# Differential attention: the tail's norm in two groups of heads, the projection begun with six heads, and items two rounds behind the units

## What is computed

```python
qkv = jnp.einsum('bld,de->ble', x, w_in)
q, k, v = jnp.split(qkv, 3, axis=-1)        # 8 heads; q and k in two halves of 64, v of 128
...
s = jnp.einsum('bqhcd,bkhcd->bhcqk', qblk, k) * scale
s = s - slopes[None, :, None, None, None] * dist
p = jax.nn.softmax(s, axis=-1)
a = p[:, :, 0] - lam * p[:, :, 1]
o = jnp.einsum('bhqk,bkhe->bqhe', a, vf)
...
o = o * lax.rsqrt(jnp.mean(o * o, -1, keepdims=True) + SUBLN_EPS) * subln_g * (1.0 - lam_init)
return jnp.einsum('ble,ed->bld', o, w_o)
```

## Time and profile before

| | |
|---|---|
| time, median of 3 runs | 2782.74 us (2771.02 to 2784.29) |
| time of the profiled execution | 2781.65 us |
| its span in the trace | 2779.6 us |
| TensorE / VectorE / ScalarE busy | 94% / 73% / 55% |
| start of the scores of item 21, the first behind the last unit | 120.34 us |
| start of the projection | 150.87 us |
| end of the projection, start of the norm's sums | 177.04 us |

### The profile page before, as it was taken

How to read it: one execution, slowest core, us unless ns; L and a number is a source line. 1 busy time by engine, 2 the same in 40 slices (tenths; PEclk the granted TensorE clock), 3 DMA queues, 4 the chain that set the end, 5 groups by cost and what they waited for, 6 DMA issues and landing times. The chain is left out here.

```text
span 2779.6 us, 48273 instructions
## 1 busy us (share of the span) xinstructions
PE 2601.0 (94%) x20505; PEld 2138.3 (77%) x20505; DVE 2017.6 (73%) x2876; ACT 1534.7 (55%) x2217; POOL 128.9 (5%) x176
## 2 busy tenths in 40 slices
PE   8899999998997999999999999998999889999888
PEld 7689987787965666666666666666969779979778
DVE  7755558654356989889898989896757865757864
ACT  5544425221124877777777778775446444546443
POOL 0000000010004000000000000000200101100101
PEclk9999999999997999999999999999999999999999
DMA  6325433100033989899999989893625534625532
GB/s 193 97 73 185 162 117 116 61 4 3 4 135 118 367 331 365 332 347 349 345 351 347 350 330 365 332 365 105 197 74 167 175 104 145 196 76 167 166 105 101
DMA packets 250985, 550.43 MB, mean 198 GB/s; under 512 B 25549, under 2 KB 193157, under 8 KB 207629
## 3 DMA queue, kind: packets, MB, share of 16 engines
q1 hardware_dynamic: 246796, 541.52, 56.1%
q0 software_dynamic: 3968, 5.78, 0.7%
HBM read 540.43 MB, written 1.05 MB: 195 GB/s over the span
## 5 line engine op out<-in xcount | busy, mean ns | idle before, releaser
L316 DVE TENSOR_TENSOR wl<-raw,wh 128x1024 fp32r<-128x1024 f32 (+1 forms) x610 | 742.6, 1221 | 341.8 <-ACT wh L307 324.1
L307 ACT ACTIVATE wh<-raw 128x1024 fp32r<-128x1024 f32 (+1 forms) x610 | 640.5, 1053 | 485.0 <-PE PS L163 434.0
L316 DVE TENSOR_TENSOR wl<-early,wh 128x1024 fp32r<-128x1024 f32 x384 | 466.8, 1225 | 55.6 <-ACT wh L307 35.3
L307 ACT ACTIVATE wh<-early 128x1024 fp32r<-128x1024 f32 x384 | 407.0, 1061 | 128.0 <-PE PS L163 118.7
L161 PE MATMUL PS<-wh,xe_h 128*96 128x512 f32 x896 | 357.2, 399 | 1.2 <-DVE xe_l L2018 1.2
L161 PE MATMUL PS<-b_hn_h,wh 128*128 128x256 f32 (+1 forms) x1152 | 336.9, 292 | 22.1 <-DVE wl L316 15.9
L163 PE MATMUL PS<-wh,xe_l 128*96 128x512 f32 x896 | 353.6, 395 | 0.0
L162 PE MATMUL PS<-wl,xe_h 128*96 128x512 f32 x896 | 353.6, 395 | 0.0
L162 PE MATMUL PS<-b_hn_l,wh 128*128 128x256 f32 (+1 forms) x1152 | 329.6, 286 | 0.0
L163 PE MATMUL PS<-b_hn_h,wl 128*128 128x256 f32 (+1 forms) x1152 | 329.4, 286 | 0.0
L161 PEld LDWEIGHTS PS<-b_hn_h,wh 128*128 128x128 f32 (+1 forms) x1152 | 223.0, 194 | 28.4 <-DVE wl L316 18.3
(11 more groups left out here) (473 smaller groups left out, 5046.8 us busy)
## 6 DMA issues: line engine op xcount, KB each, us to landing
early<-in_moe_in SPq DMA_DIRECT2D x128, 1024.0 KB, 5.0
raw<-in_moe_in SPq DMA_DIRECT2D x96, 1024.0 KB, 4.9
raw<-in_w_in SPq DMA_DIRECT2D x76, 1024.0 KB, 5.4
early<-in_moe_out SPq DMA_DIRECT2D x64, 1024.0 KB, 4.9
raw<-in_moe_out SPq DMA_DIRECT2D x48, 1024.0 KB, 5.0
raw<-in_attn_w_in SPq DMA_DIRECT2D x24, 512.0 KB, 5.8
raw<-in_rw_w_rkv SPq DMA_DIRECT2D x12, 1024.0 KB, 5.0
raw<-in_ffn_w_gate SPq DMA_DIRECT2D x11, 1024.0 KB, 5.5
```

The source lines that it names most:

```text
L307: act.e.activation(st.two(n)[0], st.raw(n), ACT.Copy).then_inc(*act.sig("hi", st.name, n, sem=f"hi_{st.name}"))
L316: dve.e.tensor_tensor(lo, st.raw(n), hi.bitcast(F32), SUB).then_inc(*dve.sig("lo", st.name, n, sem=f"lo_{st.name}"))
```

## The change

It has three parts. First, items run two rounds behind the units, not three: n = i - 2, with `unit(i)` written ahead of `scores(n)`, and the loop is three rounds shorter in its count. Second, the norm over heads is done in two groups: heads 0 to 5 (bank 6, `n_0`, `r_0`), whose root is taken while items 22 and 23 are still at work, and heads 6 and 7 (bank 7, `n_1`, `r_1`), whose root is taken during the projection. Third, the projection starts when the first rows of group 0 are there; the sum of squares of head 7 stands behind its first row of the contraction, the spreads of heads 6 and 7 behind its fifth. The four unused matmuls go, and PSUM banks are named by hand.

```diff
--- before.py
+++ after.py
@@ -528,7 +528,7 @@
     at_t = [tile3(f"at_t{n}", 3, T) for n in range(2)]
     at_x = [tile(f"at_x{n}", 8) for n in range(NP_)]
     lam_m, lam = tile("lam_m", 64), tile("lam", 4)
-    at_sq, n8, r8 = tile3("at_sq", KC, T), tile("n8", T)[0:8], tile("r8", T)[0:8]
+    at_sq, n8, r8 = tile3("at_sq", KC, T), *([tile(f"{x}8_{g}", T)[0:8] for g in (0, 1)] for x in "nr")
     at_xs = two("at_x", KC, T)
     at_u = [tile(f"at_u{n}", T) for n in range(2)]
     ITEMS = [(h, i) for h in range(8) for i in range(3)]
@@ -536,19 +536,19 @@
     def attention_order(unit, v_turned, scores, turned, values, sums):
 
 
-        for i in range(len(UNITS) + 8):
-            n = i - 3
+        for i in range(len(UNITS) + 5):
+            n = i - 2
+            if i < len(UNITS):
+                unit(i)
             if 0 <= n < len(ITEMS):
                 scores(n)
-            if i < len(UNITS):
-                unit(i)
             if i >= 3 and i % 3 == 0 and i <= len(UNITS):
                 v_turned(i // 3 - 1)
             if n >= 5 and n % 3 == 2 and n // 3 <= 8:
                 values(n // 3 - 1)
             if 2 <= n < len(ITEMS) + 2:
                 turned(n - 2)
-            if n >= 7 and n % 3 == 1 and n // 3 <= 9:
+            if n >= 7 and n % 3 == 1:
                 sums(n // 3 - 2)
 
     def attention_pe(pe):
@@ -609,25 +609,39 @@
             t.then_inc(*pe.sig("attn_v_mm", h))
 
         def sums(h):
-            if h == 0:
-                bank("subln", b=6)
+
+            g, r = h // 6, h % 6
+            if r == 0:
+                b, before = bank("subln", g, b=6 + g)
+                if before:
+                    pe.wait_ge(pe.at(*before))
             pe.wait_ge(pe.at("at_sq", h))
-            t = e.matmul(PS[0:8, 6, 0:T], one_of_8[:, 7 - h:15 - h], at_sq[:, h, :], start=h == 0, stop=h == 7)
-            if h == 7:
-                t.then_inc(*pe.sig("subln_mm"))
+            t = e.matmul(PS[0:8, 6 + g, 0:T], one_of_8[:, 7 - r:15 - r], at_sq[:, h, :], start=r == 0, stop=h in (5, 7))
+            if h in (5, 7):
+                t.then_inc(*pe.sig("subln_mm", g))
+
+        def spread(h):
+            g, r = h // 6, h % 6
+            pe.wait_ge(pe.at("subln_r", g))
+            b, before = bank("subln_o", h, b=h % 3)
+            pe.wait_ge(pe.at(*before))
+            e.matmul(PS[:, b, 0:T], ident[0:8, r:r + 1].to_broadcast([8, 128]), r8[g], start=True, stop=True).then_inc(
+                *pe.sig("subln_o_mm", h))
 
         attention_order(unit, v_turned, scores, turned, values, sums)
-        busy_pe(pe, 4, "subln", at=7)
-        pe.wait_ge(pe.at("subln_r"))
-        for h in range(8):
-            b, before = bank("subln_o", h)
-            pe.wait_ge(pe.at(*before))
-            e.matmul(PS[:, b, 0:T], ident[0:8, h:h + 1].to_broadcast([8, 128]), r8, start=True, stop=True).then_inc(
-                *pe.sig("subln_o_mm", h))
-        for _ in project_units(pe, SA, "attn_o", [("attn_o", i) for i in range(4)], at_xs, T, ("x_lo", "attn_o")):
+        for h in range(6):
+            spread(h)
+        rows = project_units(pe, SA, "attn_o", [("attn_o", i) for i in range(4)], at_xs, T, ("x_lo", "attn_o"), (4, 5, 6, 3))
+        next(rows)
+        sums(7)
+        for _ in range(4):
+            next(rows)
+        spread(6)
+        spread(7)
+        for _ in rows:
             pass
         for i in range(4, KC):
-            project_unit(pe, SA, "attn_o", i, 128, at_xs, T)
+            project_unit(pe, SA, "attn_o", i, 128, at_xs, T, b=(7, 0, 1, 2)[i - 4])
         norm_pe(pe, 0, "attn_o")
 
     def attention_act(act):
@@ -684,8 +698,12 @@
             act.wait_ge(act.at("attn_v", h))
             e.activation(at_sq[:, h, :], at_o[:, h, :], ACT.Square).then_inc(*act.sig("at_sq", h))
 
-        for i in range(len(UNITS) + 8):
-            n = i - 3
+        def root(g):
+            act.wait_ge(act.at("subln", g))
+            e.activation(n8[g], n8[g], ACT.Sqrt).then_inc(*act.sig("subln_root", g))
+
+        for i in range(len(UNITS) + 5):
+            n = i - 2
             if 1 <= i <= len(UNITS):
                 evacuated(i - 1)
             if i >= 4 and i % 3 == 1 and i <= len(UNITS) + 1:
@@ -698,13 +716,21 @@
                 high(act, SA)
             if 0 <= n < len(ITEMS):
                 exps(n)
-            if n >= 6 and n % 3 == 0 and n // 3 <= 9:
+            if n >= 6 and n % 3 == 0:
                 sums(n // 3 - 2)
-        act.wait_ge(act.at("subln"))
-        e.activation(n8, n8, ACT.Sqrt).then_inc(*act.sig("subln_root"))
-        for h in range(8):
+            if n == 23:
+                root(0)
+
+        def o_high(h):
             act.wait_ge(act.at("subln_o", h))
             e.activation(at_xs[0][:, h, :], at_o[:, h, :], ACT.Copy).then_inc(*act.sig("x_hi", "attn_o", h))
+        o_high(0)
+        sums(7)
+        o_high(1)
+        o_high(2)
+        root(1)
+        for h in range(3, 8):
+            o_high(h)
         for i in range(KC):
             high(act, SA)
         norm_act(act, 0, ff_x[0])
@@ -776,8 +802,19 @@
             dve.wait_ge(dve.at("attn_v_mm", h))
             e.tensor_copy(at_o[:, h, :], ps("attn_v", h)).then_inc(*dve.sig("attn_v", h))
 
-        for i in range(len(UNITS) + 8):
-            n = i - 3
+        def mean_square(g):
+            dve.wait_ge(dve.at("subln_mm", g))
+            e.tensor_scalar(n8[g], ps("subln", g, p=8), 1.0 / 128, 1e-5, MUL, ADD).then_inc(*dve.sig("subln", g))
+
+        def root(g):
+
+            dve.wait_ge(dve.at("subln_root", g))
+            e.reciprocal(r8[g], n8[g]).then_inc(*dve.own())
+            dve.wait_ge(dve.last)
+            e.tensor_scalar(r8[g], r8[g], 0.8, None, MUL).then_inc(*dve.sig("subln_r", g))
+
+        for i in range(len(UNITS) + 5):
+            n = i - 2
             if 0 <= n < len(ITEMS):
                 first(n)
             if 1 <= n <= len(ITEMS):
@@ -786,25 +823,41 @@
                 low(dve, SQ)
             elif i < len(UNITS) + 1:
                 low(dve, SA)
-            if n >= 6 and n % 3 == 0 and n // 3 <= 9:
+            if n == 23:
+                mean_square(0)
+            if n >= 6 and n % 3 == 0:
                 keep(n // 3 - 2)
-        dve.wait_ge(dve.at("subln_mm"))
-        e.tensor_scalar(n8, ps("subln", p=8), 1.0 / 128, 1e-5, MUL, ADD).then_inc(*dve.sig("subln"))
-        dve.wait_ge(dve.at("subln_root"))
-        e.reciprocal(r8, n8).then_inc(*dve.own())
-        dve.wait_ge(dve.last)
-        e.tensor_scalar(r8, r8, 0.8, None, MUL).then_inc(*dve.sig("subln_r"))
-        for h in range(8):
+            if n == 24:
+                root(0)
+
+        def scale(h):
             dve.wait_ge(dve.at("subln_o_mm", h))
             e.scalar_tensor_tensor(at_o[:, h, :], at_o[:, h, :], par("subln"), ps("subln_o", h), MUL, MUL).then_inc(
                 *dve.sig("subln_o", h))
-            if h:
-                dve.wait_ge(dve.at("x_hi", "attn_o", h - 1))
-                e.tensor_tensor(at_xs[1][:, h - 1, :], at_o[:, h - 1, :], at_xs[0][:, h - 1, :].bitcast(F32), SUB).then_inc(
-                    *dve.sig("x_lo", "attn_o", h - 1))
-        dve.wait_ge(dve.at("x_hi", "attn_o", 7))
-        e.tensor_tensor(at_xs[1][:, 7, :], at_o[:, 7, :], at_xs[0][:, 7, :].bitcast(F32), SUB).then_inc(
-            *dve.sig("x_lo", "attn_o", 7))
+
+        def o_low(h):
+            dve.wait_ge(dve.at("x_hi", "attn_o", h))
+            e.tensor_tensor(at_xs[1][:, h, :], at_o[:, h, :], at_xs[0][:, h, :].bitcast(F32), SUB).then_inc(
+                *dve.sig("x_lo", "attn_o", h))
+        scale(0)
+        keep(7)
+        scale(1)
+        o_low(0)
+        scale(2)
+        o_low(1)
+        mean_square(1)
+        scale(3)
+        o_low(2)
+        scale(4)
+        o_low(3)
+        root(1)
+        scale(5)
+        o_low(4)
+        o_low(5)
+        scale(6)
+        scale(7)
+        o_low(6)
+        o_low(7)
         for i in range(KC):
             low(dve, SA)
             residual_dve(dve, "attn_o", i)
```

## The result

| | before | changed |
|---|---|---|
| time, median of 20 runs | 2779.61 us | 2786.47 us |
| range of the runs | 2771.02 to 2784.51 | 2782.10 to 2792.66 |
| time of the profiled execution | 2781.65 us | 2788.37 us |
| its span | 2779.6 us | 2786.6 us |

The ratio is 1.0022, with a 95% interval of 1.0014 to 1.0030: slower by 0.14 to 0.30%. That is inside the 0.5% called no change, but twenty runs of each tell it from zero.

What follows compares the result with a forecast made beforehand. TensorE, busy 2601.0 of 2779.6 us, was taken as the bound. 2781.65 plus 7.2 (loop), less 1.8 or 6.3 (tail at lower or higher clock), gave 2787.1 or 2782.6 us; 2786 was taken, range 2775 to 2797.

Steps and rivals of the forecast that it cites:

- The stall in the loop: Loop, second item of five heads: TensorE waits 1.44 us for ScalarE's `at_u` before the values' transposition.
- The sum of the loop: Loop: five waits of 1.44 us, 7.2 us lost in all; no matmul added.
- The tail at the lower clock: Tail from item 21's scores: spreads start at 20.1 us against 26.67, end at 54.9; 1.8 us won.
- The sum: Whole kernel: loop's loss less tail's gain gives 2787.1 or 2782.6 us; 2786 taken, two thirds toward the former.
- the low case: Whole kernel with the tail at the lower clock: 2781.65 + 7.2 - 1.8 = 2787.1 us.
- The higher-clock case: Tail at the higher clock throughout: spreads end at 23.4 us, the end is at 50.4; 6.3 us won.
- the stall was there: Rival, loop: no stall, since ScalarE squares sooner or TensorE arrives later; 2775 to 2780 us; 12 in 100.
- The clock stayed at 1.00 in the loop: Rival, loop: the clock falls in each of five new gaps, 10.5 us more at 2.1 each, 2798 us; 8 in 100.
- The early start: Rival, tail: early projection start brings nothing, end stays at 56.70 us, time 2789; counted inside the forecast (70 in 100).

Runs made afterwards that it cites:

- keep first: Changed kernel with VectorE's copy to `at_o` (`keep`) moved ahead of the head's first item; ratio to the kernel before 0.9998, median 2778.36 us.
- late square: Changed kernel with ScalarE's square of heads 0 to 4 moved behind its `at_u` and `at_t` copies and the next round's weight; ratio to the kernel before 1.0004.

## Why the prediction was right

The median is 2786.47 against a forecast of 2786. I made the sum against the profiled time, 2781.65 + 4.35; twenty runs moved the median before to 2779.61, so the change measured 6.9 us and not 4.35. The direction and the mechanism are right; that the two totals meet within 0.5 us is luck, since two errors of about 2 us cancel. By its steps:

- *The stall in the loop*: place, cause and count as written, before the values' transposition of five heads behind ScalarE's `at_u`. Forecast 1.44 us each; the profile shows a gap of 1.38 us in the head above, and from start to start TensorE is 1.45 us late. Both edits, keep first and the late square, took it away, so this is shown and not only read.
- *The sum of the loop*: 7.2 forecast, 8.02 measured (106.17 - 98.15). The missing 0.8 is mostly what the new order costs with no wait at all: 0.63 us in the kernel with keep first (98.78 - 98.15). I had said that no matmul is added and put the rest of the order at nothing. The trace shows where it lies: with the early copy a unit takes 3.19 us (from 63.91, behind the transposition of an item, to the scores at 67.10) and not 3.11, and a head has three. Why wasn't tried.
- *The tail at the lower clock*: spreads 20.1 us behind the scores of item 21 forecast, 20.40 measured; six spreads 5.8, measured 5.74 (154.59 - 148.85); end 54.9, measured 54.99. The low part of head 4 was forecast at 34.9 and TensorE's row for it went on at 163.48 - 128.45 = 35.03. So the course of the new tail was right step by step. A gain of 1.8 was forecast, 1.71 came, but against a single trace of the old tail, which took 59.83 behind the new loop. I counted its unused matmuls as cover for root and reciprocal and didn't see that they outlasted `r` by 1.65 us. I also wrote that the clock before rose only in 144 to 146; the trace before has 1.00 in 132 to 134 too. VectorE waited 5.81 us for the sum of head 7 in the middle of its scaling, as the steps have it.
- *The sum*: I took two thirds of the way to the low case. The profiled run was all the way there: 7.2 - 1.8 = 5.4 would have been nearer to the 6.3 us of the attention (161.16 - 154.85). Of the span's 7.0 us, 0.6 lie behind the norm and are not explained; runs of one kernel differ by more.
- *The higher-clock case* of the tail, 50.4 us, was too long: with the clock high throughout it is 47.01 to 47.38. The term that was too big is the stretch ahead of the spreads. I left their start at 20.1 us, a figure worked out with matmuls at the lower clock; they start at 17.05 and 17.42. The higher clock is also where the new tail's worth is seen. In the traces of mixed clock the new tail is 1.7 us shorter, at the higher clock 3.5; the 6.3 that I gave for it compared a tail at the high clock with one at the mixed clock.
- *The rivals*: the stall was there. The clock stayed at 1.00 in the loop in spite of gaps of 1.4 us, as the row on the norm's gap had it, so the rule of the Trainium skill on short idle times ("TensorE: Matmul & The Clock Gate", section "A second HAM failure mode: psum-queue depth-cycling") did not show here. The early start brought 3.5 us at the higher clock; in the traces of mixed clock its share of the 1.7 us is not separated from that of the unused matmuls.

## What to carry to other kernels

When a stage moves one round nearer, list for each engine what now stands behind each of its waits: here one ScalarE wait of 1.80 us was harmless until a copy that TensorE needs at once stood behind it. Such a wait is best taken away at its source, by moving the late instruction into idle time that its engine has anyway. In a tail, work out the start and the end each at both levels of the clock: here the spreads started 6 us sooner and the end came 2 us sooner, partly because of the clock and partly because work had moved from in front of the start to behind it. Unused matmuls in TensorE's waits helped when they fitted (54.99 to 51.19 us), and they cost time when they outlasted what they covered (1.65 us in the kernel before).

## What the runs showed of the hardware

- Spreads whose operands have eight rows kept TensorE busy (4.96 of 5 us) but did not hold its granted clock here. Behind six of them that began at 1.00 it was 0.66 over 5 us and the projection's first row took 3.00 us; with 128 rows, mostly zeros, it stayed at 1.00 and the row took 1.79. The edit was worth 2.3 us on top of the others (49.67 to 47.38), and 3.75 us alone. Both operands got 128 rows at once, so which of them counts is not shown.
- Gaps of 1.4 us between dense stretches, five times, left the granted clock at 1.00 (20 to 120 us of the changed kernel); behind the one of 3.92 us in the tail it was 0.62 in the window 134 to 136:

```profile
132.00:134.00 2.00, 0.00 (x0) 0.00 (x0) 2.00 (x4) 0.20 (x2) 0.00 (x0) 1.00 0.11 35
134.00:136.00 2.00, 1.41 (x7) 1.06 (x8) 1.76 (x6) 2.00 (x6) 0.00 (x0) 0.62 0.00 0
```
